# A softmax pipeline with one step instead of two between exponentials and scaling

## What is computed

```
proj = u @ w_in                                   # split into the columns of the three groups
ya = swa_sink_attention(...)   # A: 8 heads, window of two 64-chunks, learned sinks, rotary positions
yb = s5_mixer(...)             # B: complex diagonal state space, GELU, GLU
yc = fox_attention(...)        # C: 4 heads, causal, logits biased by cumulated forget gates
y = concat(rms_norm(ya), rms_norm(yb), rms_norm(yc)); m = y @ w_out
```

## Time and profile before

| | |
|---|---|
| median of 3 runs | 1901.37 us (1900.83 to 1903.24) |
| the profiled execution's own time | 1902.85 us |
| its span | 1901.0 us |
| TensorE busy | 1869.0 us (98%) |
| VectorE busy | 986.6 us (52%) |
| ScalarE busy | 710.7 us (37%) |
| GpSimd busy | 204.5 us (11%) |
| mean granted TensorE clock | 0.996 |
| the attention steps of layer 0 and layer 1 | about 447 to 549 and 1381 to 1484 us |

### The profile page before, as it was taken

How to read it: one execution, slowest core, us unless ns; L and a number is a source line. 1 busy time by engine, 2 the same in 40 slices (tenths; PEclk the granted TensorE clock), 3 DMA queues, 4 the chain that set the end, 5 groups by cost and what they waited for, 6 DMA issues and landing times.

```text
span 1901.0 us, 25245 instructions
## 1 busy us (share of the span) xinstructions
PE 1869.0 (98%) x9472; PEld 1544.2 (81%) x9472; DVE 986.6 (52%) x1350; ACT 710.7 (37%) x1112; POOL 204.5 (11%) x420
## 2 busy tenths in 40 slices
PE   8999999999999999999999999999999999999998
PEld 7888888887668888888888888889876788888887
DVE  5664442387667544442376544325876574444323
ACT  5332332254654333332253323223656453333321
POOL 2741000013100000000047110000130000000000
PEclk9999999999999999999999999999999999999999
DMA  6334333243213333333333443333511323333331
GB/s 181 103 115 129 95 113 105 75 139 112 57 56 89 92 97 99 99 111 102 92 103 94 139 101 100 109 102 103 158 52 50 90 67 100 99 94 106 107 92 44
DMA packets 330957, 188.61 MB, mean 99 GB/s; under 512 B 6996, under 2 KB 325432, under 8 KB 329848
## 3 DMA queue, kind: packets, MB, share of 16 engines
q1 hardware_dynamic: 324008, 168.13, 30.7%
q0 software_dynamic: 5824, 18.79, 3.4%
q10 hardware_dynamic: 1040, 0.52, 0.1%
HBM read 175.72 MB, written 11.67 MB: 99 GB/s over the span
## 4 chain that ended last, share of the span: by engine, by line
PE 91%; DVE 6%; ACT 2%; issue 1%; DMA 0%; DVEq 0%; ACTq 0%
PE ps L590 18%; PE ps L592 18%; PE ps L591 18%; PE ps L792 8%; PE ps L790 8%; PE ps L791 8%; PE ps L646 1%; PE ps L648 1%; PE ps L653 1%; PE ps L750 1%; PE ps L749 1%; PE ps L751 1%; PE ps L620 1%; PE ps L631 1%; PE ps L622 1%
## 5 line engine op out<-in xcount | busy, mean ns | idle before, releaser
L1643 DVE TENSOR_TENSOR wl<-raw,wh 128x1024 fp32r<-128x1024 f32 (+1 forms) x260 | 344.5, 1326 | 738.3 <-ACT wh L1152 737.4
L590 PE MATMUL ps<-xh,wh 128*128 128x512 f32 x1536 | 606.7, 395 | 7.5 <-DVEq L1881 6.3
L592 PE MATMUL ps<-xh,wl 128*128 128x512 f32 x1536 | 599.0, 390 | 0.0
L591 PE MATMUL ps<-xl,wh 128*128 128x512 f32 x1536 | 598.5, 390 | 0.0
L1152 ACT ACTIVATE wh<-raw 128x1024 fp32r<-128x1024 f32 (+1 forms) x260 | 295.8, 1139 | 637.7 <-PE ps L792 324.6
L590 PEld LDWEIGHTS ps<-xh,wh 128*128 128x128 f32 x1536 | 289.2, 188 | 72.8 <-DVEq L1881 7.9
L592 PEld LDWEIGHTS ps<-xh,wl 128*128 128x128 f32 x1536 | 288.7, 188 | 61.0
L591 PEld LDWEIGHTS ps<-xl,wh 128*128 128x128 f32 x1536 | 289.1, 188 | 60.1 <-issue 1.7
L790 PE MATMUL ps<-Hh,wh 128*128 128x512 f32 x638 | 248.4, 389 | 0.0
L792 PE MATMUL ps<-Hh,wl 128*128 128x512 f32 x638 | 248.2, 389 | 0.0
L791 PE MATMUL ps<-Hl,wh 128*128 128x512 f32 x638 | 248.2, 389 | 0.0
(11 more groups left out here) (382 smaller groups left out, 2038.9 us busy)
## 6 DMA issues: line engine op xcount, KB each, us to landing
raw<-in_ffn_up SPq DMA_DIRECT2D x88, 512.0 KB, 3.8
raw<-in_ffn_down SPq DMA_DIRECT2D x64, 704.0 KB, 4.5
raw<-in_ffn_gate SPq DMA_DIRECT2D x87, 512.0 KB, 3.9
raw<-in_w_in SPq DMA_DIRECT2D x28, 512.0 KB, 4.0
raw<-in_w_out SPq DMA_DIRECT2D x16, 512.0 KB, 3.7
xrow<-in_x SPq DMA_DIRECT2D x2, 1024.0 KB, 8.6
ssm_t<-evict POOLq DMA_DIRECT2D x8, 256.0 KB, 3.2
ssm_v<-evict POOLq DMA_DIRECT2D x8, 256.0 KB, 2.7
```

The costliest lines, as they stand in the source:

```text
L590: pe.matmul(bank, w_tile(True, slot, kw), xh[:, kx, :], start=first, stop=False)
L591: pe.matmul(bank, w_tile(True, slot, kw), xl[:, kx, :], start=False, stop=False)
L592: return pe.matmul(bank, w_tile(False, slot, kw), xh[:, kx, :], start=False, stop=last)
L1643: V.tensor_tensor(w_low(slot, k0, nk), raw[:, slot4, 0:nk - k0, :], w_high(slot, k0, nk).bitcast(F32), ALU.subtract).then_inc(w_split, 1)
```

## The change

One line: the three lags are each one step shorter. `PROBS` stays at three buffers, the tables of fixed work stay as they are.

```
-LAG_N, LAG_T, LAG_PV = 2, 3, 4
+LAG_N, LAG_T, LAG_PV = 1, 2, 3
 PROBS = 3
```

## The result

The kernel with the change takes 1909.16 us (median of 6 runs, 1907.31 to 1913.83) against 1901.38 us before (6 runs beside it): a ratio of 1.0042, 95% interval 1.0032 to 1.0052. It is slower, as forecast, and 2 us above the predicted median. The profiled execution happens to be the fastest of the six: 1907.31 us around a span of 1905.5.

A forecast was written before the change was run, and what follows sets the result against it. TensorE was taken to bound the kernel, with only its idle time able to change. Two layers at +2.1 gave +4.2 us, plus 1.6 for the clock: 1902.85 became 1908.7, the median 1907.2 us, range 1901.0 to 1911.5.

The forecast's parts named there:

- the clock: Attention stages: one clock drop more behind TensorE's longer idle stretches, +1.6 us; bounds -1.6 to +4.7.
- 4, bank of qc0: Step 4: value product 0 moves inside TensorE's 1.34 us wait for the bank of qc0, -0.6 us a layer.
- 12, GLU: Step 12: the GLU's wait for pair 3's output goes, as ScalarE copies it one step sooner, -0.6 us a layer.
- 13, branch sum: Step 13: value product 8 no longer covers the branch-sum wait and scaling 12 is one block wider, +0.5 us a layer.
- 14 to 19: ScalarE and VectorE run late up to the first output slice, +1.3 us a layer; bounds 0 to 2.4.
- tail: End of the stage: one of two waits ahead of transposes 23 remains, -0.5 us a layer; bounds -0.7 to +0.5.
- waits held to stay: TensorE's other bank waits at L590 keep their cover and stay, 0 us.
- Step 1, the price: VectorE's scaling 0, held up by GpSimd, delays vc0's read-out and TensorE's step 2: +2.0 us a layer; bounds +0.65 to +3.3.
- Rival (a): Attention stages: every long idle stretch drops the clock, four drops instead of one, 1910.3 us; chance 0.18.
- Rival (b): Step 1: GpSimd does not hold up scaling 0, price 0.65 us, no further clock drop, 1902.9 us; chance 0.25.
- Rival (c): All 7.1 us of probT waits at L1004 go, without ScalarE and VectorE slipping: faster, 1895.9 us; chance 0.12.

## Why the prediction was right, and where its sizes were off

The direction and the places held. The sizes did so only in part: the stalls were forecast at 4.2 us and are 2.9, the clock at 1.6 and is 4 to 5, more than all stalls together. The two misses go opposite ways, so that the total is only 2 us low is in part luck. By the steps of the prediction, in layer 0:

| step | forecast | measured in the traces |
|---|---|---|
| 2, scaling ahead of vc0's read-out | +2.0 | 0 to 1.89 |
| 4, bank of qc0 | -0.6 | 1.34 to 0.73 |
| 12, GLU | -0.6 | 0.58 to 0 |
| 13, branch sum | +0.5 | 0.96 to 1.55 |
| 14 to 19 | +1.3 | 2.25 to 3.25 |
| tail | -0.5 | 2.28 to 1.64 |
| waits held to stay (scores of step 2, products and bank of steps 9 and 10) | 0 | 1.19 to 0.89 |
| sum | +2.1 | +1.4 |

**Step 1, the price.** Right to 0.2 us (the projection's part starts 1.8 us later, and its wait is 1.89), and by the mechanism: the new rows are those of the scaling's old place, moved against GpSimd's instructions. Both of VectorE's instructions end at a fixed distance behind the end of GpSimd's: the add at 0.01 us, the multiply at 0.54 as before. By the Trainium skill's rule ("SBUF — State Buffer", section "SBUF: two separate sides") the one that comes second is blocked for the whole instruction of the other. The trace agrees that both are held until GpSimd's instruction is over, but both end some 0.15 us sooner than their own 0.16 and 0.69 us behind it; so the prediction's "the trace agrees for the add" hides the same difference as for the multiply. No run leaves GpSimd's rotation out, so its part rests on these ends alone. The run with the scaling alone shows that nothing else makes this stall, and the pair with step 19 filled that it is worth 3.6 us in two layers.

**Steps 4, 12 and 13.** As forecast; the changes came from the moved products and pair outputs, as the run that moves only the scaling lacks them.

**Steps 14 to 19.** The mechanism forecast was there, 0.3 us smaller. ScalarE's copy of step 14 comes at 518.21 us with the change, at 514.84 before; 1.56 us of that is the clock drop behind step 2 in this execution (from the start of step 2's projection part to the state-space output TensorE needed 7.73 us, and 6.17 at full clock in layer 1), which leaves 1.8 for the forecast 2.4. In step 16 VectorE's scaling waits for the exponentials, as forecast:

```profile
518.21 0.49 ACT L1421 ACTIVATE probT<-ps 128x384 f32<-128x384 f32 x1 [3.68 <-PE ps L972]
```

```profile
522.82 0.16 DVE L1992 RECIPROCAL stat<-stat 128x1 f32<-128x1 f32 x1 [1.35 <-ACT prob L1410]
```

From there ScalarE works up to its split at 528.47 with one longer pause, 1.05 us for VectorE at 527.93 (0.26 before), and the first output slice waits for the low half, as the prediction said, and as much for the copy of the values, which it had not named. That ScalarE loses time by waiting for transposes ahead of its exponentials is shown by turning the two round: 2.4 us less in two layers by the estimate, 3.1 by the two kernels that differ in this (and in three useless matmuls). By the waits, about half of it is in steps 14 to 19 and the rest in step 10.

**The clock.** This term failed in its size. I took one drop more, +1.6 us; it is 4 to 5: of the 7.8 us by which the change is slower, 2.6 to 2.9 are stalls, and with the idle stretches filled the change wins 5.3 us and the kernel before 1.1 (not clear of noise). Rival (a), a drop behind every long stretch, was nearer to it in time than the forecast, though no profile here shows its four drops: that of the change has two in four such stretches, and with the read-out first the loss was made of longer drops. The price of 1.6 us for one drop was right; the two stretches it was read from are 65.05 and 66.62 us long, not 465.05 and 466.62 as the prediction says. The reason for my small number was layer 0 of the one profiled execution, where 1.5 us of idle time passed without a drop; single executions differ, and the profiled one of the change is the fastest of its six. The stalls, smaller than forecast, hid a part of the miss.

Rival (b) fell: GpSimd did hold the scaling up. Rival (c) was half right: 5.5 of the 7.1 us at L1004 did go, but came back at L972 and L590 in the same steps, where ScalarE and VectorE owe the same work as before.

## What to carry to other kernels

A lag in a software pipeline is also a place in each queue: before shortening it, look at what stands behind the moved instruction in the same step, above all the release of a buffer, and put the release first. Where TensorE sets the end and idle stretches like those here (1.5 to 1.9 us) can't be avoided, count the clock with them, and try to fill them with work of no use; with the change that was worth more than all its stalls together, with the kernel before it was not clear of noise, and step 2 filled alone won nothing. When runs of one kernel spread by several microseconds, look at span less what the clock lost before judging an edit: two edits that removed waits looked useless until the clock was held up. Then measure with the clock held up, for the estimate is rough: both kernels that only fill step 19, or steps 2 and 19, come out 1 to 1.5 us higher by it than the change, with the same waits.

## What the runs showed of the hardware that was not expected

A drop of the clock can last much longer than in the profiles of the two kernels. With vc0 read out first, TensorE ran ten microseconds at half clock in steps 19 to 21 of layer 0 (0.53 in the mean from 528 to 538 us), though it was busy for 9.81 of these 10 us, and its mean clock was 0.992 or 0.993 in all five runs. The two kernels with less idle time had more of it: the other, with the exponentials first, had 0.991 in half of its runs, against 0.992 to 0.995 with the change. Fourteen small matmuls a layer with the read-out first, and eleven with both edits, took the mean clock back to 0.996 to 0.998.

A drop can also come where TensorE isn't idle at all. In layer 1, far ahead of the attention steps, where the change alters nothing, the kernel before runs 32 small matmuls (L706, 128x32) for 3.98 us from 1085.99 us, and the clock falls toward their end:

```profile
1086.00:1088.00 2.00, 2.00 (x20) 2.00 (x19) 0.67 (x1) 1.06 (x1) 0.00 (x0) 1.00 0.27 79
1088.00:1090.00 2.00, 2.00 (x16) 2.00 (x16) 1.16 (x2) 0.63 (x1) 0.00 (x0) 0.79 0.07 20
1090.00:1092.00 2.00, 2.00 (x5) 1.58 (x6) 0.00 (x0) 0.38 (x1) 0.77 (x2) 0.50 0.82 241
```

Seven of the twelve profiles have this drop, before and change among them; of the five without it four are of kernels with step 19 filled. So a part of the spread between executions, and perhaps of the 5.3 us, comes from outside the attention steps; how large it is in the runs without a profile isn't known.
